# Moving the last slice of a query tile behind the first transposes of probabilities in an attention stage

## What is computed

```python
def swa_sink_attention(hn, w_q, sinks, w_o, k, v):
    q = (hn @ w_q).reshape(B, nc, CHUNK, N_KV_HEADS, GROUP, HEAD_DIM)
    ...
    s = jnp.einsum('bcqkgd,bcwkd->bckgqw', q, kw) * (HEAD_DIM ** -0.5)
    ...
    m = jnp.maximum(jnp.max(s, axis=-1, keepdims=True), sink)
    p = jnp.exp(s - m)
    p = p / (jnp.sum(p, axis=-1, keepdims=True) + jnp.exp(sink - m))
    o = jnp.einsum('bckgqw,bcwkd->bcqkgd', p, vw)
    return o.reshape(B, S, N_Q_HEADS * HEAD_DIM) @ w_o
```

## Time and profile before

| | |
|---|---|
| three runs | 1111.16, 1112.71 and 1113.22 us |
| median | 1112.71 us |
| profiled execution | 1111.33 us |
| its span in the trace | 1109.5 us |
| PE busy | 1093.1 us of the span (99%) |
| DVE busy | 780.9 us (70%) |
| ACT busy | 557.0 us (50%) |
| mean granted clock of PE | 0.996 |

### The profile page before, as it was taken

The page is one execution under the profiler, slowest core; times in us unless marked ns, Lnnn a source line. Parts: engine busy times, 40 slices in busy tenths (PEclk is TensorE's granted clock), DMA queues, the critical chain, the costliest instruction groups (busy, mean ns, idle before and its releaser), DMA issues.

```text
span 1109.5 us, 17385 instructions
## 1 busy us (share of the span) xinstructions
PE 1093.1 (99%) x6901; PEld 977.4 (88%) x6901; DVE 780.9 (70%) x1117; ACT 557.0 (50%) x980; POOL 14.9 (1%) x34
## 2 busy tenths in 40 slices
PE   8999999999999999999999999999999999999998
PEld 7887787889899999988888888879899999998886
DVE  5788985778688888853347888558788888863334
ACT  6377474555355555532236576545355555542223
POOL 1000000000000000000020000000000000000000
PEclk9999999999999999999999999999999999999999
DMA  6332233234133323333333132122233333333211
GB/s 203 111 91 68 84 98 119 92 90 138 42 111 115 111 85 110 134 116 100 104 80 76 39 97 57 39 76 84 88 115 114 96 95 115 115 133 98 100 50 76
DMA packets 150962, 107.22 MB, mean 97 GB/s; under 512 B 23922, under 2 KB 140770, under 8 KB 150883
## 3 DMA queue, kind: packets, MB, share of 16 engines
q1 hardware_dynamic: 150882, 106.12, 31.7%
HBM read 104.01 MB, written 2.10 MB: 96 GB/s over the span
## 4 chain that ended last, share of the span: by engine, by line
PE 93%; DVE 4%; ACT 2%; DMA 1%; issue 0%; POOL 0%; SPq 0%; DVEq 0%
PE ps L1758 11%; PE ps L1760 11%; PE ps L1762 11%; PE ps L1536 10%; PE ps L1537 10%; PE ps L1540 10%; PE ps L1517 9%; PE ps L1518 8%; PE ps L1519 8%; PE ps L1689 1%; PE ps L1862 1%; PE ps L1889 1%; DVE w_lo L976 1%; DVE work L1166 1%; ACT junk L562 1%; DVE h L1168 1%
## 5 line engine op out<-in xcount | busy, mean ns | idle before, releaser
L976 DVE TENSOR_TENSOR w_lo<-raw,w_hi 128x1024 fp32r<-128x1024 f32 x113 | 140.4, 1245 | 166.5 <-ACT w_hi L558 166.3
L558 ACT CAST w_hi<-raw 128x1024 fp32r<-128x1024 f32 x114 | 118.9, 1046 | 168.9 <-PE ps L1540 147.5
L1517 PE MATMUL ps<-x_hi,w_hi 128*128 128x512 f32 (+1 forms) x520 | 180.8, 348 | 4.9 <-DVE w_lo L976 4.2
L1518 PE MATMUL ps<-x_lo,w_hi 128*128 128x512 f32 (+1 forms) x520 | 177.5, 341 | 0.0
L1519 PE MATMUL ps<-x_hi,w_lo 128*128 128x512 f32 (+1 forms) x520 | 177.4, 341 | 0.0
L1758 PE MATMUL ps<-t_hi,w_hi 128*128 128x256 f32 x576 | 163.5, 284 | 0.2
L1760 PE MATMUL ps<-t_lo,w_hi 128*128 128x256 f32 x576 | 163.4, 284 | 0.0
L1762 PE MATMUL ps<-t_hi,w_lo 128*128 128x256 f32 x576 | 163.4, 284 | 0.0
L1536 PE MATMUL ps<-w_hi,t_hi 128*128 128x512 f32 x352 | 137.3, 390 | 0.0
L1537 PE MATMUL ps<-w_lo,t_hi 128*128 128x512 f32 x352 | 137.3, 390 | 0.0
L1762 PE MATMUL ps<-x_hi,w_lo 128*128 128x256 f32 x432 | 122.5, 284 | 0.0
(11 more groups left out here) (202 smaller groups left out, 2011.0 us busy)
## 6 DMA issues: line engine op xcount, KB each, us to landing
raw<-in_ffn_w_gu SPq DMA_DIRECT2D x88, 512.0 KB, 4.0
raw<-in_ffn_w_down SPq DMA_DIRECT2D x44, 512.0 KB, 3.3
raw<-in_a_w_in SPq DMA_DIRECT2D x24, 512.0 KB, 4.3
raw<-in_a_w_out SPq DMA_DIRECT2D x12, 512.0 KB, 3.5
raw<-in_b_w_q SPq DMA_DIRECT2D x16, 256.0 KB, 3.4
raw<-in_b_w_o SPq DMA_DIRECT2D x16, 256.0 KB, 3.8
h<-in_x SPq DMA_DIRECT2D x4, 512.0 KB, 5.8
result<-h SPq DMA_DIRECT2D x3, 512.0 KB, 2.6
```

The costliest lines, as they stand in the source:

```text
L558: nc.scalar.copy(w_hi[:, t % 4, :], raw[:, t % 4, :]).then_inc(w_hi_ready, 1)
L976: v.tensor_tensor(w_lo[:, t % 4, :], raw[:, t % 4, :], w_hi[:, t % 4, :].bitcast(F32), ALU.subtract)\
L1517: nc.tensor.matmul(out_ps, hi_w, hi_x, start=first, stop=False)
L1518: nc.tensor.matmul(out_ps, hi_w, lo_x, start=False, stop=False)
```

## The change

The slices 5 to 7 of the third query tile (m = 2) stood ahead of the first pair's transposes. Now slices 5 and 6 stay there, and slice 7 comes behind the transposes, ahead of the first pair's value products. No instruction is added or dropped on any engine, and only PE's order changes.

```diff
             turn_v()
             queries(2, range(0, 5))
             scores(1)
-            queries(2, range(5, DC))
+            queries(2, range(5, DC - 1))
             turn_p(0)
+            queries(2, range(DC - 1, DC))
             values(0)
             for m in range(1, PAIRS_H - 2):
                 scores(m + 1)
```

## The result

The changed kernel is slower, by 0.24%. Its median is 1115.38 us over 20 runs (1110.77 to 1117.15), against 1112.51 us over 20 runs of the kernel before; the ratio is 1.0024 with a 95% interval of 1.0016 to 1.0031. The profiled execution took 1115.59 us with a span of 1113.8. The forecast was 1111.9 us, with 1113.9 as the upper end of its range.

A forecast was written before the change was run, and what follows sets the result against it. PE, busy 99% of the span, was taken as the bound, with VectorE's chain deciding in steps two and three. Of 0.31 us gained, 0.25 remained: 1112.1 - 0.25 = 1111.9 us, range 1110.3 to 1113.9.

The forecast's parts named there:

- The first transposes at 631.72: First pair's transposes on PE start at 631.72 instead of 632.03, 0.31 us earlier, waiting for ScalarE's half of the division.
- The first value products 0.31 us earlier with 0.35 us of idle left: First value products start at 634.17 instead of 634.48; moved products fill PE's 1.08 us idle except about 0.35 us.
- The exponentials near 637.5: ScalarE's exponentials of the second pair start near 637.5 instead of 637.72, after a row maximum 0.25 us earlier.
- The clock stays up at 636: Three more full products may keep PE's clock up where it fell to half at 636, worth 3.2 us of PE's work.
- PE waits for VectorE in step two, 1.2 and 1.7 us: If the clock holds, PE stands 1.2 us before the second transposes and 1.7 us before the second value products.
- So the 3.2 us of clock come back as stalls, and 0.25 us remain: VectorE's chain sets the third value products at 660.24 whatever the clock does, so only 0.25 us is gained.
- a low clock behind 648: Sign that the prediction is wrong: PE's clock low after 648, in or after the second step.
- The rival with the right mechanism, place and sign: Slower: new stalls around the second transposes make the clock fall near 649; third value products 2.4 us later, 1114.5 us; chance 0.08.
- The base: Starting time of the forecast: 1112.1 us, the mean of one profiled and three unprofiled runs of the kernel before.
- clock costs vary: Rival: low clock starts later or lasts longer in some executions, and the change removes that loss too: 1110.9 us; chance 0.14.

The follow-up runs named there:

- the fills: Changed kernel plus idle products in step two's stalls: four before second transposes and six before second value products, 1112.16 us; the six alone, 1112.53 us.
- the doubled change: Against the kernel before, the last two slices of the third query tile, not one, moved behind the first transposes: 1111.76 us, ratio 1.0001.
- the filled old order: Kernel before, order untouched, plus six idle products in front of the second step's value products: 1114.25 us, ratio 1.0012.
- VectorE's order turned: Changed kernel without filling; in step two VectorE does the low half of the probabilities ahead of the next row maximum: 1112.85 us, ratio 1.0006.

## Why the prediction was wrong, point by point

- The first transposes at 631.72, bound by ScalarE's division: right. The division ends at 630.32 + 1.49 = 631.81, and they start 0.10 us later, 631.71 with the offset taken off. The stall in front is 0.30 us, not 0.4, and the profile names no engine for it (`issue`); that it is the division rests on the times.
- The first value products 0.31 us earlier with 0.35 us of idle left: right in the time (0.35 us, offset taken off); the idle left is 0.18 us instead of 0.35. The moved products start where they were reckoned, within 0.05 us (633.19 and 633.75, less the offset); only the time at which the array is free behind them came later, at 633.95 instead of 633.8.
- The exponentials near 637.5: 637.66, less the offset 637.46. Right.
- The clock stays up at 636: thought likely, and right. The moved slice does that, and three idle products do it too. The Trainium skill (TensorE: Matmul & The Clock Gate, Part 4: PE-mode transpose) says that transposes don't count as activity the way matmuls do. The traces are in line with it: with the same transposes, the clock fell or held according to whether three products stood behind them. No run leaves the transposes out, so that they are the reason for the fall isn't shown.
- PE waits for VectorE in step two, 1.2 and 1.7 us: right. 1.12 and 1.60 us were measured, and the fills show that it is time to spare, since 2.3 us of added work vanish in it.
- "So the 3.2 us of clock come back as stalls, and 0.25 us remain": this is the step that failed. It holds only if the clock survives those stalls. Where it does, the sum is right: the attention takes 80.87 to 80.89 us up to the sixth step against 81.14 before, and the two changed runs of 20 with a mean clock of 0.999 are at 1110.77 and 1111.17 us. In the other 18 it fell. In the trace it fell at 649.4, and from the second to the third value products PE took 16.13 us instead of the 11.32 reckoned with. The prediction had named this sign of being wrong, a low clock behind 648; in its sum the path through step two has the clock either falling at 636 or not at all.
- The rival with the right mechanism, place and sign was on record with a chance of 0.08. Two things in it were mis-sized. Its chance: against it stood the stall of 0.60 us at 699.40, after which the clock stayed up, at 1.00 in every window to 708. That was a weak comparison. That stall is much shorter than 1.2 and 1.7 us, and behind those transposes follow full products of 128x512; behind the stall at 649 follow 24 short value products and the scores. The nearer row was the fall of the trace itself: 1.08 us of idle, and then the same short value products. Which of the two counts, the length of the stall or what follows it, isn't shown; in the doubled change the clock fell among full products, behind a stall of 1.58 us. Its price: I took 3.2 us from a low stretch of under 7 us. The one at 649 lasts 10 us and costs 16.13 - 11.32 = 4.8 us. PE was 0.55 us ahead at the second value products, and the old kernel took 11.46 us for the stretch behind them, 0.14 us more than PE needs. Less these 0.7 us, that is the 4.1 us seen.
- The base. The kernel before isn't one time but a fall in every run: all 35 runs of the last comparison have mean clocks of 0.996 or less. Where the fall is short it costs nothing (81.14 us up to the sixth step with it and 81.13 to 81.14 without), since PE gives up time that it would have stood for VectorE; those runs lie at 1111.2 to 1111.9, or 1.9 us above. Where it is long, as in the profile of the filled old order, it costs about 1.2 us, if the groups are read rightly: eleven of the 35 lie at 1112.3 to 1112.7. This was the premise of the rival "clock costs vary", and it fits the runs of the kernel before. But the long stretch was traced only in the old order with six idle products, and the kernel before has one trace, with the short one.

So the change exchanges a fall that costs nothing where it is short, at 636 with a wait for VectorE still ahead, for one at 649 with that wait just behind it.

What stays open: why some runs with the stall of 1.6 us unfilled had no fall. Of the changed kernel, the one with only the transposes' stall filled and the old order with three idle products, 31 of 35 runs have a mean clock of 0.996 or less and four have 0.999; with the stall filled, wholly or in part, all 66 runs of six kernels have 0.999 or more. Open too is what decides between a short and a long low stretch.

## What to carry to other kernels

When an engine waits for another in the next stage, time won ahead of that wait is worth little, here 0.25 of 3.5 us, and on PE it can be worth less than nothing: the wait gets longer, and the clock can fall behind it. So where a step saves PE time, look up what PE then stands in front of, and compare that place with the place in the trace where the clock did fall, products ahead and behind included. A few idle products in a wait that can't be removed were free here, and 0.7 us of them were enough; the same products where PE has no wait cost their full time. And where single runs scatter by more than the change is worth, compare a stretch of the trace that leaves the scatter out: 81.14 against 80.87 us told what the medians couldn't.

## What the runs showed of the hardware

- The clock fell with no idle of PE longer than 1.60 us anywhere near (1.08 us in the old order), and stayed up over 1.12 us in front of transposes when the next gap was filled. It can also stay up over both gaps unfilled: it did over 1.02 and 1.62 us in the profile of the old order with three idle products.
- Low stretches came in lengths of about 3.4 us (VectorE's order turned, and the doubled change), 6.8 us (the kernel before) and 10 us (the changed kernel). The lengths follow from the windows: a window of 2 us with a mean of 0.59 was low for 1.6 of them.
- A fall may cost nothing: the attention of the old order, up to its sixth step, takes 81.14 us with a low stretch of 6.8 us and 81.13 to 81.14 with none, though PE needs 3.2 us more for its work in it.
- The level of the clock at the first tile, at 12 us, is worth 2.0 us, and the granted clock in the windows doesn't show it (1.00 from 12 to 16 us in both groups); the distance between products does (0.12 or 0.21 us for 128x256).
- An addition of two 128x1024 operands on VectorE took 1.23 us with GpSimd at rest and 2.09 us with a multiplication of the same size running on GpSimd across half of it.
